# A decoder layer on one core: a third ready-made u tile in each attention head, at other places, and two joints in another order

## The chip, the core and the metric

The kernel runs on one core of a Trainium2 chip. The metric is the device time of one execution in microseconds (us). TensorE is called PE, VectorE DVE, ScalarE ACT, GpSimd POOL and SyncE SP; SP does nothing but issue DMAs here. PE, DVE, ACT and POOL work in parallel, each in its own program order, and wait for each other by semaphores.

## What is computed

```python
h = rms(x, attn_norm_g)
q, k, v, cb, cc, cx = split(h @ w_in[l])             # 512 tokens, D = 2048, float32
a = diff_attention(rms(q), rms(k), v, lam)           # 8 heads, causal, ALiBi
c = cb * causal_conv3(cc * cx)                       # 1024 channels
x = x + concat(rms(a) * (1 - lam_init), c) @ w_out[l]
h2 = rms(x, ffn_norm_g)                              # PEER: 128 x 128 experts, 8 heads, top 16
act = gelu(sum(u[experts] * h2)) * gates
x = x + sum(act * v[experts])
```

Float32 products are made from three float32r products each: an operand is split in a high part (ACT copies it) and a low part (DVE subtracts), and PE multiplies high x high, low x high and high x low.

## The kernel before

**Stages.** In time: the projection to q, k, v (to about 289 us); the head loop, 8 trips of attention together with one eighth of the convolution's projection (to about 620); the output projection (to 800); h2, its transposition and the first queries (to 867); the sweep (to 2219), which multiplies all 128 tiles of 128 experts' u rows with h2 for 384 of the 512 tokens, while DVE does the remaining 128 tokens with gathered rows; and the dense second half with v.

**The u tiles.** A tile is 128 rows of 2048 floats, 1 MB, and must be transposed for PE. In the sweep an ordinary tile is loaded by SP into one of two buffers (`u_tile`), PE turns it in 16 steps of 128 x 128 into PSUM (`turned`, 8 steps after each half of the tile before), ACT and DVE split it from PSUM (`split_u`), and PE multiplies. 56 of the 128 tiles, the odd ones up to 111, are ready-made: in stage one, where DVE is idle at times, SP loads the rows into `near_rows` (or `far_rows`), DVE turns them in four instructions (`turn_rows`) into `near_turned`, and four DMAs of 256 KB (`store_turned`) put the result into `uT_all` in DRAM. The sweep loads such a tile from there, PE turns nothing, and ACT and DVE split it from SBUF. `turned_before(tile)` says which tiles these are. There is one near buffer for rows and one for the turned tile, so a row load waits for the turning before it (`seg_ready`), and a turning waits for its rows (`seg_in`) and for the stores of the one before (`seg_kept` in the heads, where POOL issues the stores, else `seg_stored`).

**A sweep head** is 16 tiles. In heads 0 to 5 PE also makes the queries of a later head, behind tiles 3 to 6 and 9 to 12; DVE chooses the experts of the next head in heads 0 to 6, and does a `dot` and an `add` per tile.

**A trip of the head loop.** PE does the convolution's products, `conv(0)`, `conv(1)`, `conv(2)`, with attention's small products between their parts. The convolution's weights come in six pieces (0 to 5) a head of 512 KB, through two raw buffers `wc_raw`; SP issues piece p + 2 when DVE has split piece p (`wc_ready`). DVE's order is: split piece 3, piece 4, `biased` and `combined` for the four query blocks (scores plus bias and maximum; after ACT's exponentials the combination), split pieces 5 and 0, last combination, split piece 1, norms, `o_n`, `norm_qk`, split piece 2, the conv gate (lines 1461 to 1470). Of the two turnings in a trip, the first is cut in two behind `combined(0)` and `combined(1)`, the second sits between `o_n` and `norm_qk`. SP issues their row loads in

```python
if p in (2, 5):
    next_rows(NEAR, 2 * j + (NEAR_HEADS + p // 5))
```

behind weight pieces 4 and 1. POOL issues in a trip two 1 MB DMAs that fill a grid in DRAM with zeros (`zero_cells`), the head's outputs, the stores of the turned tiles (line 455), and does the roots of the norms. SP's DMAs are queue q1 in the profile, POOL's are q0, ACT's q10.

**The joints.** Into the head loop: ACT splits weight pieces 0, 1 and 2 and then copies two of the four blocks of the last projection chunk (`keep_qkv`), DVE the two others; PE waits for all four before the first convolution product. At h2: PE turns h2 in four blocks of 16 steps (`turn_rows`, line 1797) into PSUM banks 4 to 7, each bank waiting until DVE (`low`) has read the block before.

## Time and profile before

| | us |
|---|---|
| median of 3 runs | 2975.82 (2974.24 to 2977.21) |
| the profiled execution | 2978.89 |
| its span, first to last instruction | 2977.1 |
| PE busy | 2893.4 (97%) |
| DVE busy | 2358.1 (79%) |
| POOL busy | 1518.6 (51%) |
| ACT busy | 1049.6 (35%) |
| moved by DMA | 980.65 MB, 329 GB/s |

Busy times are those of the engines' instructions; matmuls overlap each other, and their ends are modelled, so that a busy PE isn't one at its peak. Idle time is counted just ahead of an instruction and put down to what released it. The share of DMA is the mean busy share of the core's 16 DMA engines.

### The profile page before, as it was taken

How to read it: one execution, taken by the hardware profiler on the slowest of the kernel's cores; microseconds unless marked ns; L12 is line 12 of the kernel's file. 1: busy time of each engine (PE TensorE's matmuls, PEld its weight loads, DVE VectorE, ACT ScalarE, POOL GpSimd, SP SyncE). 2: the span in 40 equal slices, each digit the busy share in tenths (PEclk: the TensorE clock that was granted, in tenths of full speed). 3: DMA queues.
4: the chain of work that ended last, by engine and by line, in shares of the span. 5: the costliest groups of instructions: out<-in, count | busy, mean ns of one | idle time of the engine just before them, and what ended most of it. 6: DMA issues, size and time to landing. Idle time of an engine off the chain costs nothing.

```text
span 2977.1 us, 40581 instructions
## 1 busy us (share of the span) xinstructions
PE 2893.4 (97%) x14993; PEld 2571.8 (86%) x14993; DVE 2358.1 (79%) x3050; ACT 1049.6 (35%) x1373; POOL 1518.6 (51%) x906
## 2 busy tenths in 40 slices
PE   7999999999999999999999999999999999999998
PEld 6887777778889999999999999999998777777777
DVE  6445677755678888988888898899778888899898
ACT  4111433341323343434333343334234333333333
POOL 1000232200015666666666666566868877788752
PEclk9999999999999999999999999999999999999999
DMA  8998777779758998999899898999999999999998
GB/s 298 338 347 273 236 238 236 226 298 314 241 183 304 315 344 296 348 309 331 311 321 339 300 346 312 329 347 355 326 370 390 415 414 414 408 416 416 414 416 343
DMA packets 333295, 980.65 MB, mean 329 GB/s; under 512 B 63764, under 2 KB 180512, under 8 KB 241760
## 3 DMA queue, kind: packets, MB, share of 16 engines
q1 hardware_dynamic: 188560, 508.60, 46.6%
q0 software_dynamic: 107008, 439.75, 41.0%
q10 hardware_dynamic: 37584, 30.43, 3.2%
q8 instruction: 86, 1.41, 0.2%
q14 instruction: 57, 0.47, 0.0%
HBM read 866.33 MB, written 112.33 MB: 329 GB/s over the span
## 4 chain that ended last, share of the span: by engine, by line
PE 63%; DVE 14%; DMA 12%; issue 5%; ACT 3%; POOL 2%; SPq 0%; ACTq 0%; DVEq 0%; POOLq 0%
PE ps L1803 19%; PE ps L1805 19%; PE ps L1804 19%; DMA v_raw<-in_peer_v 9%; PE ps L2053 3%; DVE x_rows L1663 3%; DVE u_row L1654 2%; DMA wc_raw<-in_w_in 2%; DVE v_lo L1703 2%; ACT v_hi L1174 1%; POOL dots L824 1%; POOL v_ring L835 1%; DVE uT_lo L1643 1%; DVE near_turned L1296 1%; DVE uT_lo L1648 1%
## 5 line engine op out<-in xcount | busy, mean ns | idle before, releaser
L1803 PE MATMUL ps<-hT_hi,uT_hi 128*128 128x384 f32 x2048 | 698.9, 341 | 10.5 <-DVE uT_lo L1643 8.8
L1805 PE MATMUL ps<-h2T_lo,uT_hi 128*128 128x384 f32 x2048 | 686.1, 335 | 0.0
L1804 PE MATMUL ps<-hT_hi,uT_lo 128*128 128x384 f32 x2048 | 684.9, 334 | 0.0
L816 POOL DMA_INDIRECT gate_grid<-gates,grid_cells x256 | 547.0, 2137 | 107.4 <-issue 78.8
L1803 PE MATMUL ps<-v_hi,a_hi 128*128 128x512 f32 x1024 | 404.8, 395 | 37.3 <-DVE v_lo L1703 36.6
L1174 ACT ACTIVATE v_hi<-v_raw 128x2048 fp32r<-128x2048 f32 x128 | 245.6, 1919 | 458.3 <-PE ps L1805 348.0
L1804 PE MATMUL ps<-v_hi,a_lo 128*128 128x512 f32 x1024 | 402.9, 393 | 0.0
L1805 PE MATMUL ps<-v_lo,a_hi 128*128 128x512 f32 x1024 | 402.6, 393 | 0.0
L1803 PEld LDWEIGHTS ps<-hT_hi,uT_hi 128*128 128x128 f32 x2048 | 384.8, 188 | 19.1 <-DVE uT_lo L1643 14.8
L1804 PEld LDWEIGHTS ps<-hT_hi,uT_lo 128*128 128x128 f32 x2048 | 385.0, 188 | 1.9
L1805 PEld LDWEIGHTS ps<-h2T_lo,uT_hi 128*128 128x128 f32 x2048 | 384.3, 188 | 0.0
L835 POOL DMA_INDIRECT v_ring<-in_peer_v,experts x128 | 285.5, 2230 | 144.8 <-DVE x_one L1753 113.5
L1703 DVE TENSOR_TENSOR v_lo<-v_raw,v_hi 128x2048 fp32r<-128x2048 f32 x128 | 293.2, 2290 | 74.5 <-ACT v_hi L1174 74.3
L1753 DVE SCALAR_TENSOR_TENSOR x_one<-v_ring,acts,x_one 128x2048 f32<-128x2048 f32 x128 | 300.4, 2347 | 6.9 <-DMA v_ring<-in_peer_v,experts 4.1
L1663 DVE SCALAR_TENSOR_TENSOR x_rows<-v_row,acts,x_rows 128x2048 f32<-128x2048 f32 x128 | 300.0, 2344 | 1.9 <-ACT acts L1127 1.5
L806 POOL DMA_INDIRECT v_row<-in_peer_v,experts x128 | 139.4, 1089 | 315.9 <-DVE x_rows L1663 266.6
L1654 DVE CUSTOM_DVE_ANT_0 u_row<-u_row,h_rows 128x2048 f32<-128x2048 f32 x128 | 292.5, 2285 | 5.9 <-DMA u_row<-in_peer_u,experts 5.9
L824 POOL DMA_INDIRECT dots<-products_one,cells x128 | 258.1, 2016 | 43.4 <-issue 38.7
L1803 PEld LDWEIGHTS ps<-v_hi,a_hi 128*128 128x128 f32 x1024 | 195.0, 190 | 85.7 <-issue 30.1
L1118 ACT ACTIVATE uT_hi<-ps 128x1024 fp32r<-128x1024 f32 x144 | 148.1, 1029 | 310.5 <-PE ps L2053 304.2
L1648 DVE TENSOR_TENSOR uT_lo<-ps,uT_hi 128x1024 fp32r<-128x1024 f32 x144 | 176.1, 1223 | 99.7 <-ACT uT_hi L1118 98.2
L801 POOL DMA_INDIRECT u_row<-in_peer_u,experts x128 | 181.7, 1419 | 123.1 <-DVE dots L1654 49.4
(207 smaller groups left out, 5036.6 us busy)
## 6 DMA issues: line engine op xcount, KB each, us to landing
v_raw<-in_peer_v SPq DMA_DIRECT2D x128, 1024.0 KB, 14.9
u_tile<-in_peer_u SPq DMA_DIRECT2D x72, 1024.0 KB, 7.2
u_tile<-uT_all SPq DMA_DIRECT2D x56, 1024.0 KB, 6.7
near_rows<-in_peer_u SPq DMA_DIRECT2D x40, 1024.0 KB, 8.2
uT_all<-near_turned SPq DMA_DIRECT2D x100, 256.0 KB, 7.0
w_raw<-in_w_in SPq DMA_DIRECT2D x24, 1024.0 KB, 9.1
wc_raw<-in_w_in SPq DMA_DIRECT2D x48, 512.0 KB, 7.4
far_rows<-in_peer_u SPq DMA_DIRECT2D x16, 1024.0 KB, 9.0
```

What stands on the lines that cost most here:

```text
L816: pool.indirect_dma_start(out=gate_grid, out_offset=bass.IndirectOffsetOnAxis(ap=grid_cells[:, d, col:col + 1], axis=0), in_=gates[:, 2 + ...
L824: pool.indirect_dma_start(out=dots[:, s:s + 1], out_offset=None, in_=products_one, in_offset=bass.IndirectOffsetOnAxis(ap=cells[:, col:col ...
L835: pool.indirect_dma_start(out=v_ring[s % RING][:, :], out_offset=None, in_=v_table, in_offset=slot(1, h, s)).then_inc(v_in[s % RING], 16)
L1174: nc.scalar.activation(v_hi[b % 2][:, :], v_raw[b % RAW_RING][:, :], ACT.Copy).then_inc(v_hi_ready, 1)
L1648: v.tensor_tensor(uT_lo[half][:, :, :], ps_uT[half], uT_hi[half][:, :, :].bitcast(F32), ALU.subtract)\
L1654: v.tensor_tensor_reduce(out=u_row[c % 2][:, :], in0=u_row[c % 2][:, :], in1=h_rows[:, 0, :], scale=1.0, scalar=0.0, op0=ALU.mult, op1=ALU ...
L1663: v.scalar_tensor_tensor(out=x_rows[:, 0, :], in0=v_row[c % 2][:, :], scalar=acts0[:, b:b + 1], in1=x_rows[:, 0, :], op0=ALU.mult, op1=ALU ...
L1703: v.tensor_tensor(v_lo[b % 2][:, :], v_raw[b % RAW_RING][:, :], v_hi[b % 2][:, :].bitcast(F32), ALU.subtract).then_inc(v_lo_ready, 1)
L1753: v.scalar_tensor_tensor(out=x_one[:, :], in0=v_ring[s % RING][:, :], scalar=acts[:, s:s + 1], in1=x_one[:, :], op0=ALU.mult, op1=ALU.add) ...
L1803: mm(out, a_hi, b_hi, start=first, stop=False)
L1804: mm(out, a_lo, b_hi, start=False, stop=False)
L1805: return mm(out, a_hi, b_lo, start=False, stop=last)
```

## The change

It makes 63 tiles ready instead of 56. The seven new ones are tile 6 of each sweep head 0 to 6 (`EXTRA_AT = 6`), turned in heads 0 to 6 of the head loop, three near tiles in a trip instead of two. In the trip the first turning is whole and sits behind `combined(1)`; the second sits behind `combined(3)`; the third at the trip's end, behind the conv gate. The row loads are issued behind weight pieces 5, 0 and 1. POOL stores the third one at the beginning of the next trip, ahead of the zero fill. In the sweep, `u_tile[0]` now holds a ready-made tile too. At the first joint ACT splits piece 2 behind its two copies, and PE waits for one of the four blocks at first and for the others ahead of `conv(1)`. At h2, block 1 is turned into banks 0 to 3, after the last output sum has been added from each, and its splits come ahead of the last block's square and mean.

```diff
-KEPT_BY_POOL = 1 + 2 * (HEADS - 1)
+EXTRA = HEADS - 1
+EXTRA_AT = 6
+KEPT_BY_POOL = 1 + 3 * (HEADS - 1)
...
 def turned_before(tile):
-    return tile % 2 == 1 and tile < 2 * TURNED
+    if tile % TOPK == EXTRA_AT:
+        return tile // TOPK < EXTRA
+    return tile % 2 == 1 and tile < 2 * ODD_TURNED
+def kept_row(tile):
+    return ODD_TURNED + tile // TOPK if tile % TOPK == EXTRA_AT else tile // 2
...
+        def turned_bank(n, t, b):
+            return ps[:, b if (n, t) == (1, 1) else 4 + b, :]
...
                     sp.wait_ge(wc_ready, PIECES * j + p + 1)
                     conv_piece(j + (p + 2) // PIECES, (p + 2) % PIECES)
-                    if p in (2, 5):
-                        next_rows(NEAR, 2 * j + (NEAR_HEADS + p // 5))
+                    if p >= 3:
+                        then = (odd_of_head(j, 1), odd_of_head(j, 2), extra(j))[p - 3]
+                        next_rows(3 * j + (NEAR_HEADS + p - 3), then[0])
...
             for j in range(HEADS):
+                if j > 0:
+                    keep_turned(NEAR_HEADS + 3 * j, extra(j - 1))
                 for n in range(2 * j, 2 * j + 2):
                     zero_cells(n)
                 if j > 0:
                     store_o(j - 1)
                 if j < HEADS - 1:
-                    keep_turned(NEAR_HEADS + 1 + 2 * j)
+                    keep_turned(NEAR_HEADS + 1 + 3 * j, odd_of_head(j, 1))
+                    keep_turned(NEAR_HEADS + 2 + 3 * j, odd_of_head(j, 2))
...
-                    keep_turned(NEAR_HEADS + 2 + 2 * j)
...
-            for p in range(PIECE_RING):
+            for p in range(PIECE_RING - 1):
                 split_wc(0, p)
             keep_qkv(chunks - 1)
+            split_wc(0, PIECE_RING - 1)
...
             high(1, 0)
+            high(1, 1)
             square(1, 3)
-            for t in range(1, TB):
+            for t in range(2, TB):
                 high(1, t)
...
                 combined(0)
-                if not last:
-                    turn_rows(NEAR, 2 * j + (NEAR_HEADS + 1), "heads", range(2))
                 biased(2)
                 combined(1)
                 if not last:
-                    turn_rows(NEAR, 2 * j + (NEAR_HEADS + 1), "heads", range(2, 4))
+                    turn_rows(NEAR, 3 * j + (NEAR_HEADS + 1), "heads")
...
                 combined(3)
                 if not last:
+                    turn_rows(NEAR, 3 * j + (NEAR_HEADS + 2), "heads")
                     split_wc(j + 1, 1)
...
                 if not last:
-                    turn_rows(NEAR, 2 * j + (NEAR_HEADS + 2), "heads")
                     norm_qk(j + 1, 1)
...
                 dve.wait_ge(conv_out, j + 1)
+                if not last:
+                    turn_rows(NEAR, 3 * j + (NEAR_HEADS + 3), "heads")
...
             low(1, 0)
+            low(1, 1)
             mean(1, 3)
-            low(1, 1)
...
-            for t in range(TB):
-                pe.wait_ge(proj_kept[t], QKV_CHUNKS)
+            pe.wait_ge(proj_kept[0], QKV_CHUNKS)
...
-                if not first:
+                if first:
+                    for t in range(1, TB):
+                        pe.wait_ge(proj_kept[t], QKV_CHUNKS)
+                else:
                     pe.wait_ge(conv_gated, j)
                 conv(1, 1, 0, 4)
```

Left out are the renamed arguments of the loads and stores (a tile and a row of `uT_all` in place of a count), and the two views of `u_tile`.

## Rows read from the trace of the kernel before

**Rows 1.** Busy time by stage: length, then PE, PEld, DVE, ACT, POOL busy; clock; DMA.
```profile
290.00:330.00 40.00, 37.54 (x174) 29.45 (x175) 23.69 (x57) 14.96 (x31) 9.13 (x11) 0.96 0.65 202
371.00:413.00 42.00, 41.54 (x206) 32.83 (x205) 30.47 (x66) 16.75 (x34) 11.67 (x14) 1.00 0.76 241
790.00:870.00 80.00, 71.71 (x417) 61.29 (x416) 59.27 (x154) 28.51 (x43) 9.34 (x8) 1.00 0.51 180
1210.00:2215.00 1005.00, 998.22 (x5948) 973.23 (x5947) 858.25 (x1240) 373.26 (x596) 654.97 (x387) 1.00 0.94 330
```

**Rows 2.** What PE waited for in the whole span: us, times, longest.
```profile
PE ps L1803 <- DVE uT_lo L1643: 8.8, 14, 1.3
PE ps L1797 <- DVE h2T_lo L1244: 3.6, 2, 2.1
PE ps L1803 <- ACT qkv L900: 3.6, 1, 3.6
```

**Rows 3.** DVE in order of time, one head of the head loop: start, us, instruction.
```profile
378.64 2.48 DVE L1296 STREAM_TRANSPOSE near_turned<-near_rows 128x512 f32<-128x512 f32 x4
383.40 0.69 DVE L1461 TENSOR_TENSOR conv_u<-ps,c_sb 128x512 f32<-128x512 f32 x1
387.67 1.23 DVE L1264 TENSOR_TENSOR wc_lo<-wc_raw,wc_hi 128x1024 fp32r<-128x1024 f32 x1 [0.53 <-DVE b_sb L1470]
400.32 1.30 DVE L1296 STREAM_TRANSPOSE near_turned<-near_rows 128x512 f32<-128x512 f32 x2
420.23 2.48 DVE L1296 STREAM_TRANSPOSE near_turned<-near_rows 128x512 f32<-128x512 f32 x4
```

**Rows 4.** The columns of rows 1, over one quarter of that head.
```profile
387.70:400.30 12.60, 12.14 (x59) 8.81 (x58) 9.15 (x29) 5.73 (x16) 2.61 (x4) 1.00 1.04 382
```

**Rows 5.** ACT in order of time: tile ends in sweep heads 6 and 7.
```profile
1963.70 0.49 ACT L1148 ACTIVATE products<-ps 128x384 f32<-128x384 f32 x1 [3.13 <-PE ps L1805]
1972.92 0.49 ACT L1148 ACTIVATE products<-ps 128x384 f32<-128x384 f32 x1 [3.10 <-PE ps L1805]
...
2109.15 0.50 ACT L1148 ACTIVATE products<-ps 128x384 f32<-128x384 f32 x1 [3.14 <-PE ps L1805]
2119.25 0.50 ACT L1148 ACTIVATE products<-ps 128x384 f32<-128x384 f32 x1 [3.14 <-PE ps L1805]
```

**Rows 6.** The columns of rows 1: tile 6 of head 3; two tiles of head 6.
```profile
1449.00:1461.00 12.00, 12.00 (x69) 11.48 (x68) 9.35 (x17) 2.96 (x5) 7.22 (x5) 1.00 1.02 388
1963.20:1982.30 19.10, 18.71 (x114) 18.33 (x113) 17.99 (x29) 6.05 (x10) 12.51 (x8) 1.00 0.94 347
```

**Rows 7.** DVE in order of time, sweep head 6: second half of tile 6.
```profile
1966.26 1.23 DVE L1648 TENSOR_TENSOR uT_lo<-ps,uT_hi 128x1024 fp32r<-128x1024 f32 x1 [0.28 <-ACT uT_hi L1118]
```

**Rows 8.** SP's issues in order of time: the row load of that head.
```profile
384.37 1.92 SPq L469 DMA_DIRECT2D near_rows<-in_peer_u  x1
```

**Rows 9.** DMA, 393 to 398 us: queues (packets, MB, share); issue, KB, us to landing.
```profile
q0 software_dynamic: 460, 1.77, 87.6%
q1 hardware_dynamic: 449, 0.26, 16.4%
wc_raw<-in_w_in SPq DMA_DIRECT2D x1, 512.0 KB, 9.2
```

**Rows 10.** DMA, 388.5 to 390 us: the weight piece issued just ahead of that.
```profile
wc_raw<-in_w_in SPq DMA_DIRECT2D x1, 512.0 KB, 12.5
```

**Rows 11.** DMA, 449.9 to 451.5 us: row load, weight piece, no POOL traffic.
```profile
near_rows<-in_peer_u SPq DMA_DIRECT2D x1, 1024.0 KB, 7.0
...
wc_raw<-in_w_in SPq DMA_DIRECT2D x1, 512.0 KB, 7.7
```

**Rows 12.** DMA, 403 to 408 us: the stores of a turned tile, alone.
```profile
q0 software_dynamic: 320, 1.05, 81.5%
uT_all<-near_turned POOLq DMA_DIRECT2D x3, 256.0 KB, 4.4
```

**Rows 13.** ACT in order of time: its half of a weight piece's split.
```profile
391.31 1.06 ACT L911 ACTIVATE wc_hi<-wc_raw 128x1024 fp32r<-128x1024 f32 x1 [2.37 <-DMA wc_raw<-in_w_in]
```

More of the change, by code:

```diff
@@ L335, in decoder_layer @@
         ps_key_scores = [ps[:, 7 - c, :].rearrange("p (t n) -> p t n", t=TB) for c in range(2)]
[L336 removed]
+        uT_rows = [u_tile[b][:, :].rearrange("p (a k e) -> p k a e", a=QUADS, e=QUAD) for b in range(2)]
         ps_uT = [ps[:, 2 * i:2 * i + 2, :].rearrange("p b (k e) -> p (b k) e", k=4) for i in range(2)]
@@ L488, in load_qkv_weights, with keep_odd @@
             def load_qkv_weights():
+                def keep_odd(pair, n, last=False):
+                    keep_turned(pair, n, odd(pair, n), None if last else odd(pair, n + 1))
                 def chunk(c, first=False):
@@ L524, in far, with keep_odd @@
                     return FAR_QKV + 2 * c
+                def keep_odd(pair, n, last=False):
+                    seen = EXTRA if pair == NEAR else 0
+                    keep_turned(pair, n, odd(pair, n - seen), None if last else odd(pair, n - seen + 1))
                 for q in range(1, 4):
```

101 lines of the change are left out of this document (54 added, 47 removed).

## The prediction

> **What bounds the kernel now.** I read the busy time by stage first [rows 1]. The reader is to see that PE is the bound nearly everywhere the change works: 41.54 of 42 us in a head of the head loop, 998 of 1005 us in the sweep. DVE is next, 30.47 of 42 and 858 of 1005. Two places leave PE idle, the entry of the head loop (37.54 of 40 us, granted clock 0.96) and the turning of h2 before the sweep (71.71 of 80). What PE waited for [rows 2] names them: 3.6 us for ACT's copy of the projection, 3.6 us in two waits for h2T_lo, and in the sweep 8.8 us for uT_lo of tiles that come ready-made. So a PE instruction removed from the sweep is time won, unless DVE cannot follow; DVE work added to the heads is hidden as long as it, and the transfers it hangs on, fit in 41.6 us, the step from one turning to that of the next head [rows 3]. The DMA engines are the third resource: in a head they are busy for 0.76 of the time on the mean [rows 1], but for 1.04 between 387.7 and 400.3 us [rows 4], which is full.
>
> **Part one, the sweep.** An ordinary tile costs PE 16 turnings, 8 after each half. The step between tile ends is 10.10 us in the last sweep head, where every tile has all 16, and 9.22 us for tile 6 of head 6, whose interval has 8 [rows 5]. So 8 turnings are 0.88 us and a tile 1.76 us. ACT and DVE do the same splits from the tile in SBUF as they did from PSUM. In sweep heads 0 to 5 the intervals of tiles 5 and 6 fall from 12.0 to 11.1 us each, while DVE is busy for 9.35 us in that of tile 6 [rows 6]; it follows, and the whole 1.76 is won. In head 6 it doesn't: DVE is busy 17.99 of 19.1 us over two tiles [rows 6], the gaps between its short instructions fill the rest, and the one real gap is the 0.28 us ahead of tile 6's second half [rows 7]. That gap is what can go there. Sum: 6 x 1.76 + 0.3 = 10.9 us won. The load of tile 8 now waits for DVE's last split of tile 6, some 3 us later than for PE's turnings, and has more than a tile of slack.
>
> **Part two, the heads.** A third tile a head adds to DVE one turning of 2.5 us [rows 3], to DMA 1 MB of rows and 1 MB of stores, and it moves the other two. By DVE's busy time alone, 30.5 + 2.5 of 41.6 us, it is free. But one buffer for rows and one for the turned tile serve all three, so the steps form a loop, and the new places set its order. Per head: turn n1 (ahead of the scores of the fourth block), its four stores, turn n2 (behind the last combination, ahead of the split of weight piece 1 of the next head), SP's row load for n3 and, behind it in SP's order, piece 2 of the next head; its split; the conv gate; turn n3 at the head's end; the split of piece 3; and only then, behind piece 5 in SP's queue, the row load for the next n1. Before, that load was issued one piece earlier, at 384.4, ahead of the full stretch [rows 8]. SP's waits for a turning also hold back the weight pieces now.
>
> What a load costs in the full stretch is in the trace. From 393 to 398 us the POOL queue (q0) moved 460 packets and SP's (q1) 449: one for one, but 1.77 MB against 0.26 MB, since weight pieces go in short packets [rows 9]. The piece issued just before took 12.5 us [rows 10], the next, queued behind it, 9.2 [rows 9]; alone a load and a piece take 7.0 and 7.7 [rows 11]. The Trainium skill (DMA: Bandwidth & Descriptors, Queues, rings and completion order) says the same of every SDMA engine: it goes round the rows of rings that have work, packet by packet. By that rule SP's piece would stay slow for as long as POOL has packets left, the stores of n3 as well as the zero fill, and the rule speaks against these places.
>
> The loop, each term once. Turn n1 2.5. Its stores: 0.3 to the issue, 1.7 of issuing, 4.4 to land [rows 12], and 2.7 more because n2's rows (1.05 MB, at 382 GB/s [rows 4]) share the engines: 9.1; alone 6.4. Turn n2 2.5. Piece 2 behind the rows of n3: 1.1 to its issue and 7.7 [rows 11], plus 2.8 of the 4.1 us of engine time of n2's stores (81.5% of 5 us [rows 12]), which are ahead of it: 11.6; without them 8.8. ACT's and DVE's split of it: 1.06 and 1.23, 2.3 [rows 3, 13]. Conv gate, 383.40 to 387.67: 4.3 [rows 3]. Turn n3 2.5. Split of piece 3 and SP's two issues: 2.0. Rows for n1 behind piece 5: 12.5 + 2.7 - 0.6 (they are issued 0.6 later) = 14.6 [rows 4, 10]; n3's stores are ahead of it as well but the zero fill starts later, so I add only 0.3: 14.9. At best it is the 9.2 of the queued piece [rows 9], at worst all 4.1 of the stores come on top: 18.7. The sum is 2.5 + 9.1 + 2.5 + 11.6 + 2.3 + 4.3 + 2.5 + 2.0 + 14.9 = 51.7 us. With every transfer at its lowest it is 2.5 + 6.4 + 2.5 + 8.8 + 2.3 + 4.3 + 2.5 + 2.0 + 9.2 = 40.5, under the 41.6 of PE; at the highest 55.5.
>
> I take 51.7: no row lets a load behind a weight piece, issued into the zero fill, land in 9.2 us if it has a megabyte of its own. The heads then run at the pace of the loop: +10.1 us in each of the six heads 1 to 6. Heads 0 and 7 hold only a part of the loop, and are taken at nothing. PE would wait in them mostly ahead of the third block of attention weights, since n1 sits between the second combination and the scores of the fourth block. 
>
> **Part three, the joints.** At the head loop's entry PE no longer waits for all four copies and ACT makes them before piece 2. If PE sets the time, the 3.6 us wait and the 1.6 us of low clock go: 5.2. If the loop does, PE's lead is eaten in head 0 and only DVE's start counts; I take 1.0. At h2, block 1 is turned into free banks, so the two waits of 3.6 us shrink, but DVE's four subtractions and scalings stay in series ahead of the queries: between 0 and 3.6, taken 0.6.
>
> **Sum.** 6 x 10.1 = 60.6 lost, 10.9 + 1.0 + 0.6 = 12.5 won: +48.1 us. The profiled execution took 2978.9 us (span 2977.1 and 1.8 around it), 3.1 above the median of 2975.8; it would become 3027.0, and the median 3023.9.
>
> **Rivals.** (A) The steps fit, and it ends faster. This decides at a loop of 41.6 us or less: the loads keep near their lowest bounds, because PE's and POOL's steps slide so that piece 5 no longer meets the zero fill. For it: the lowest sum is 40.5, and DVE has 11 us idle in a head. Against it: 1.04 of DMA share where the load now falls, and 2 MB more a head to move. It gives 10.9 + 5.2 + 0.6 = 16.7 won, 2959.1. (B) Only the queue order of piece 5 bites, all else is at its lowest: 40.5 + 14.9 - 9.2 = 46.2, +4.6 a head, 27.6 in all, net +15.1: 2990.9. (C) The loop passes PE by 2 us a head: 12 lost, 12.5 won, no change: 2975. (D) It doesn't do what it says: the sweep heads behave like head 6 and win 0.3 each, 2.1 in all. The first row of the tile windows speaks against it [rows 6]; it would add 8.8 to any case.
>
> **How the numbers follow.** 0.2%, 6 us, is what a measurement of this kernel can tell from no change. The forecast has 0.64, B 0.16, A 0.13, C 0.07; D is inside them. Slower 0.80, same 0.07, faster 0.13. The range runs from 2972 (a loop just above PE's, between C and A) to 3050 (a loop of 55.5: 6 x 13.9 = 83.4 lost, +70.9, and some clock loss).
>
> **What would show it.** In the changed kernel a head would take about 51 us from one turning to the next of its kind, in heads 1 to 6, and about 41.6 in head 7; DVE would be idle ahead of near_turned, released by the row load (n1) and by the stores (n2); PE idle, 60 us in all, released by DVE's probs and by splits; row loads issued behind piece 5 would take some 15 us to land. Sweep heads 0 to 5 would be 1.76 us shorter, head 6 by 0.3. Heads of 41.6 us would make the forecast wrong, and a row load landing in under 10 us would say why.

## The result, and the profile after

The changed kernel takes 3000.7 us (median of 4 runs, 2994.8 to 3001.5) against 2976.5 for the one before on the same chip (4 runs, 2974.2 to 2978.4). The ratio is 1.0074, with a 95% interval from 1.0062 to 1.0085: 22 us slower. The forecast was 3023.9, slower by 48. The side was right and the size was twice too large. The loop that the forecast describes is the one at work in the heads; one term of it was too large.

The profiled execution has a span of 2999.6 us (2977.1 before). I cut both spans at four points that are easy to find in PE's order of time: the first turning of qk_n (head 0), the first matmul of the output projection, the first of the sweep and the end of its last. An execution is one sample; the code of the last stage is the same in every kernel here, and that stage took from 749.7 to 757.7 us in their traces, so a difference of a few us there means nothing.

```
stretch, us                              before    after    change   forecast
start to the first qk turning             305.1    299.4      -5.7      -1.0
to the output projection (8 heads)        320.0    360.6     +40.6     +60.6
to the first sweep matmul                 242.0    243.2      +1.2      -0.6
first to last sweep matmul               1352.2   1340.7     -11.6     -10.9
last stage                                757.7    755.7      -2.0       0
span                                     2977.1   2999.6     +22.5     +48.1
```

So the sweep gave what it was to give, and most of the difference from the forecast, 20 of 25.6 us, lies in the heads. By head, from one first qk turning to the next, they are longer by 4.1 us in head 0 (45.0 instead of 40.9), by 34.3 in heads 1 to 6 together (5.7 each) and by 2.2 in head 7. The entry seems to have given more than forecast, but head 0 takes 4.1 of its 5.7 us back. Here are the stretches by the columns of [rows 1]: the entry, one head from the turning of n3 to the next, the turning of h2, the sweep.

```profile
290.00:330.00 40.00, 37.95 (x186) 29.50 (x186) 27.02 (x61) 15.30 (x31) 11.07 (x15) 1.00 0.75 219
392.52:440.14 47.62, 43.22 (x203) 33.29 (x202) 32.62 (x71) 16.10 (x32) 14.01 (x18) 0.96 0.78 253
810.00:890.00 80.00, 74.78 (x408) 63.41 (x407) 51.88 (x116) 29.30 (x40) 7.54 (x8) 0.98 0.43 135
1245.00:2243.00 998.00, 990.51 (x5873) 965.59 (x5872) 858.83 (x1237) 373.28 (x595) 640.85 (x387) 1.00 0.95 334
```

The entry has lost its low clock (0.96 in [rows 1], 1.00 here) and its 3.6 us wait. One head takes 47.6 us, where it took 41.6; PE is busy for 43.2 of them at a clock of 0.96, DVE for 32.6, and the DMA share on the mean is 0.78, hardly more than the 0.76 of [rows 1]. No engine is full in a head any more, so something waits. What PE waited for (us, times, longest), which answers [rows 2]:

```profile
PE ps L1933 <- DVE probs L1452: 21.4, 16, 2.5
...
PE ps L1940 <- ACT aT L1002: 10.8, 7, 2.0
PE ps L1841 <- DVE h2T_lo L1280: 1.8, 1, 1.8
```

Two entries are new or grown: probs, 2.2 us before, and aT, which wasn't there. Both lie wholly in the heads. In the head of the second line of the first fence PE's long waits are at the first block's probs and at the fourth block's aT; between them come six matmuls that start 0.43 us apart instead of 0.23 (busy 0.63 instead of 0.40, PE in order of time):

```profile
400.72 0.33 PE L1933 MATMUL ps<-ident,probs 128*128 128x128 f32 x1 [1.99 <-DVE probs L1452]
...
404.01 0.63 PE L1842 MATMUL ps<-hT_hi,wc_lo 128*128 128x512 f32 x1
...
406.49 0.40 PE L1842 MATMUL ps<-hT_hi,wc_lo 128*128 128x512 f32 x1
...
423.17 1.16 PE L1940 MATMUL ps<-qkv,aT 128*128 x8 [1.63 <-ACT aT L1002]
```

DVE and SP in the same head (start, us, instruction; idle before it and what ended that), which answer [rows 3] and [rows 8]:

```profile
392.52 2.49 DVE L1332 STREAM_TRANSPOSE near_turned<-near_rows 128x512 f32<-128x512 f32 x4 [0.25 <-DVE b_sb L1504]
...
408.10 2.49 DVE L1332 STREAM_TRANSPOSE near_turned<-near_rows 128x512 f32<-128x512 f32 x4 [3.04 <-DMA near_rows<-in_peer_u]
...
420.30 2.49 DVE L1332 STREAM_TRANSPOSE near_turned<-near_rows 128x512 f32<-128x512 f32 x4 [1.55 <-DMA uT_all<-near_turned]
...
435.01 1.23 DVE L1300 TENSOR_TENSOR wc_lo<-wc_raw,wc_hi 128x1024 fp32r<-128x1024 f32 x1 [2.11 <-ACT wc_hi L945]
...
440.14 2.49 DVE L1332 STREAM_TRANSPOSE near_turned<-near_rows 128x512 f32<-128x512 f32 x4 [0.25 <-DVE b_sb L1504]
```

```profile
397.09 0.36 SPq L494 DMA_DIRECT2D near_rows<-in_peer_u  x1
...
410.79 0.34 SPq L494 DMA_DIRECT2D near_rows<-in_peer_u  x1
...
422.99 0.35 SPq L494 DMA_DIRECT2D near_rows<-in_peer_u  x1
423.88 12.90 SPq L593 DMA_DIRECT2D wc_raw<-in_w_in  x3
```

n3 is turned at 392.5, n1 at 408.1, n2 at 420.3, n3 again at 440.1. The row load for n1 is issued at 397.1, for n2 at 410.8, for n3 at 423.0; behind the last stands weight piece 2, at 423.9. Its load takes 10.0 us, and the row load for n1 takes 10.9 (issues: KB, us to landing):

```profile
near_rows<-in_peer_u SPq DMA_DIRECT2D x1, 1024.0 KB, 10.9
...
wc_raw<-in_w_in SPq DMA_DIRECT2D x1, 512.0 KB, 10.0
```

The steps of my sum, by these rows: n1 2.5 (2.5 forecast), its stores until n2 starts 9.7 (9.1), n2 2.5, from its end to n3 17.4 (11.6 + 2.3 + 4.3 = 18.2), n3 2.5, from its end to n1 13.1 (2.0 + 14.9 = 16.9). That makes 47.6 where I had 51.7. It is the loop that I described, with one link 3.8 us shorter.

Adding up to the period proves nothing by itself, since any list of steps that closes on itself does, idle time included. What counts is that no step has slack. The profile's chain of the work that ended last (start, us, what) goes through the head before in this way, some of its pieces:

```profile
349.75 10.50 DMA near_rows<-in_peer_u
...
361.00 1.87 DVE near_turned L1332 x3
...
364.81 7.62 DMA uT_all<-near_turned
...
373.08 1.87 DVE near_turned L1332 x3
...
376.03 10.24 DMA wc_raw<-in_w_in
...
391.58 0.70 DVE b_sb L1504
```

That is the forecast's list: rows for n1, n1, its stores, n2, weight piece 2, the conv gate's last step, and then n3. This is head 1. No PE instruction is in its chain, and none in those of three others of the six heads 1 to 6; in heads 2 and 3 the chain takes a way of the same length over PE for 8.8 us, while the rows of n1 land 0.1 us before it is turned there too. The waits of DVE in all heads (us, times, longest):

```profile
DVE near_turned L1332 <- DMA near_rows<-in_peer_u: 15.7, 6, 3.0
...
DVE near_turned L1332 <- DMA uT_all<-near_turned: 12.4, 8, 2.4
```

n1 is turned within 0.2 us of the landing of its rows in six heads of seven (in head 4 n3's stores land last), n2 within 0.1 us of n1's last store in all seven, piece 2 is issued 0.7 to 1.1 us behind n2's end, and n3 follows the gate by 0.25 us each time. PE, busy for 43.2 of 47.6 us, has 4 us a head to spare, and its waits are where they show.

### The profile page after: what moved, and what is told of

It is laid out like the page before. It is cut to its first block, busy times and chain, and to the rows that moved or that the text cites. A ratio compares the mean times of both kernels' runs of the same rounds, so it can differ in the third digit from the quotient of the medians.

```text
span 2999.6 us, 40476 instructions
## 1 busy us (share of the span) xinstructions
PE 2889.1 (96%) x14881; PEld 2562.0 (85%) x14881; DVE 2373.3 (79%) x3078; ACT 1049.2 (35%) x1373; POOL 1528.3 (51%) x934
## 3 DMA queue, kind: packets, MB, share of 16 engines
q0 software_dynamic: 109248, 447.09, 40.9%
## 4 chain that ended last, share of the span: by engine, by line
PE 61%; DVE 16%; DMA 15%; issue 5%; ACT 2%; POOL 1%; SPq 0%; ACTq 0%; DVEq 0%; POOLq 0%
PE ps L1841 19%; PE ps L1843 19%; PE ps L1842 19%; DMA v_raw<-in_peer_v 9%; DVE x_rows L1699 3%; PE ps L2093 3%; DVE u_row L1690 3%; DMA wc_raw<-in_w_in 2%; DMA uT_all<-near_turned 2%; DVE v_lo L1739 2%; DVE near_turned L1332 1%; ACT v_hi L1210 1%; DMA near_rows<-in_peer_u 1%; DVE uT_lo L1679 1%; DVE uT_lo L1684 1%
## 5 line engine op out<-in xcount | busy, mean ns | idle before, releaser
L850 POOL DMA_INDIRECT gate_grid<-gates,grid_cells x256 | 536.3, 2095 | 108.7 <-issue 78.8
L840 POOL DMA_INDIRECT v_row<-in_peer_v,experts x128 | 147.4, 1152 | 318.1 <-DVE x_rows L1699 275.4
L858 POOL DMA_INDIRECT dots<-products_one,cells x128 | 271.5, 2121 | 40.9 <-issue 38.7
L480 POOL DMA_DIRECT2D uT_all<-near_turned x88 | 49.2, 567 | 425.7 <-DVE near_turned L1332 422.2
L1841 PE MATMUL ps<-w_hi,hT_hi 128*128 128x512 f32 x624 | 243.7, 390 | 1.9 <-DVE wi_lo L1286 1.9
L1842 PE MATMUL ps<-w_hi,hT_lo 128*128 128x512 f32 x624 | 243.4, 390 | 0.0
## 6 DMA issues: line engine op xcount, KB each, us to landing
v_raw<-in_peer_v SPq DMA_DIRECT2D x128, 1024.0 KB, 15.4
```

The lines of the kernel that those rows point to most:

```text
L840: pool.indirect_dma_start(out=v_row[b % 2][:, :], out_offset=None, in_=v_table, in_offset=slot(0, i, b)).then_inc(v0_in[b % 2], 16)
L850: pool.indirect_dma_start(out=gate_grid, out_offset=bass.IndirectOffsetOnAxis(ap=grid_cells[:, d, col:col + 1], axis=0), in_=gates[:, 2 + ...
L858: pool.indirect_dma_start(out=dots[:, s:s + 1], out_offset=None, in_=products_one, in_offset=bass.IndirectOffsetOnAxis(ap=cells[:, col:col ...
L1841: mm(out, a_hi, b_hi, start=first, stop=False)
L1842: mm(out, a_lo, b_hi, start=False, stop=False)
```

## The experiments

Three theories stood at the start. **T1**, the forecast's: the three tiles pass through one rows buffer and one turned buffer, and this loop of transfers, with weight piece 2 and the conv gate in it, sets the length of a head. **Order**: the new places alone cost PE waits, loop or no loop. **Contention**: the engines have too much to move in a head. A fourth, T2 to T4 in the expectations, came out of the first runs: PE sets the length, and waits for engines that weight pieces hold up. Where a sum is given for "the heads", it is the second line of the table above, read in the same way from the run's own trace.

**The joints alone** (e1). The kernel before, with the entry of the heads and the turning of h2 in the changed order and nothing else:

```diff
-            for p in range(PIECE_RING):
+            for p in range(PIECE_RING - 1):
                 split_wc(0, p)
             keep_qkv(chunks - 1)
+            split_wc(0, PIECE_RING - 1)
...
-            for t in range(TB):
-                pe.wait_ge(proj_kept[t], QKV_CHUNKS)
+            pe.wait_ge(proj_kept[0], QKV_CHUNKS)
...
-                    if t > 0:
-                        pe.wait_ge(hT_ready, 4 * (n * TB + t - 1) + b + 1)
+                    if (n, t) == (1, 1):
+                        pe.wait_ge(out_added[b], OUT_CHUNKS)
+                    elif t > 0:
+                        pe.wait_ge(hT_ready, 4 * (n * TB + (0 if (n, t) == (1, 2) else t - 1)) + b + 1)
```

> The kernel before with the two reordered joints of stage one and of h2 alone, no third tile, old places. Three theories. T (PE sets the pace of the heads, so what the entry saves is kept): in the changed kernel the first qk turning came 5.7 us earlier and the stretch from the first h2 turning to the first sweep matmul was 1.2 us longer; here the same two, so 2976.5 - 5.7 + 1.2 = 2972.0, ratio 0.9985. As forecast (the two joints are worth 1.0 and 0.6): 2974.9, ratio 0.9995. Rival (DVE's start of head 0 sets the pace, the entry's gain is eaten within a head): first qk turning 5 us earlier, but wo first matmul where it was; ratio 1.000 or 1.0004.

Measured 0.9975 (0.9965 to 0.9985), 7 us faster. The first qk turning comes 5.3 us earlier, the heads take 320.9 us (320.0 before), the next stretch 241.6 (242.0). PE sets the pace of the heads before, so the entry's gain is kept whole. What the h2 joint is worth can't be told: 0.4 us here, -1.2 in the changed kernel, while the kernels below, all with the same h2 order, took 241.4 to 243.2 in their traces.

**The third tile left out of the heads** (e2), and **the third tile on DVE alone** (e3). With both, the sweep reads the kept rows of tile 5 once more where it would read those of tile 6. In e2 the two other tiles keep their new places:

```diff
-                    if p >= 3:
-                        then = (odd_of_head(j, 1), odd_of_head(j, 2), extra(j))[p - 3]
-                        next_rows(3 * j + (NEAR_HEADS + p - 3), then[0])
+                    if p in (3, 4):
+                        next_rows(2 * j + (NEAR_HEADS + p - 3), odd_of_head(j, p - 2)[0])
...
-                if not last:
-                    turn_rows(NEAR, 3 * j + (NEAR_HEADS + 3), "heads")
```

and e3 keeps DVE's turning, with no load and no store behind it, so that it waits for those of n2 alone; the row load for the next n1 still waits for it:

```diff
-                    turn_rows(NEAR, 3 * j + (NEAR_HEADS + 3), "heads")
+                    turn_rows(NEAR, 3 * j + (NEAR_HEADS + 3), "heads", loaded=2 * j + (NEAR_HEADS + 2),
+                              kept=2 * j + (NEAR_HEADS + 3))
```

> The changed kernel without the third tile's making: in the heads it is neither loaded nor turned nor stored; tile 6 of a sweep head then reads the kept rows of tile 5 once more, so that part of the output is wrong. The two other tiles stay at their new places, joints and sweep as in the changed kernel. T (the loop of the three tiles through one rows buffer and one turned buffer sets the heads' length): heads back at 41.6 us or less, the 40.6 us lost between the first qk turning and the first output-projection matmul go, total 2976.5 - 5.7 + 1.2 - 11.6 = 2960. Rival 1 (the new places of the two tiles put their turnings ahead of the scores' readers and cost PE waits by themselves): heads of 43 to 45 us, total 2970 to 2985. It also prices the sweep alone: -11.6 us from first to last sweep matmul (forecast 10.9).

> As the run before, but DVE makes the third turning at the head's end (2.5 us) from the rows it last turned; no load and no store for it, so SP's row load for n1 still waits for that turning and stands behind piece 5, and no tile 6 is kept. T: what costs is that three tiles pass the two buffers with their transfers; with two passes left the heads stay at PE's pace, 41.6 to 42.2 us, total 2960 to 2964. Rival 1 (DVE's order: the turning at the head's end delays the conv split and the first probs of the next head, PE waits 2 us for them and falls to the low clock for 6 matmuls, as in the trace of the changed kernel): heads of 45 to 47 us, total 2985 to 2995.

e2 measured 1.0003 (0.9993 to 1.0012), its heads 340.0 us; e3 1.0041 (1.0025 to 1.0057), its heads 350.4. T1 wanted 320 to 325 for both. So the theory of the order is right as far as it goes: with the changed kernel and e1 the runs give 320.9 with the old places, 19.1 more with the new places of two tiles, 10.4 more with the third turning on DVE, 10.2 more with the third tile's own transfers. The ratios say the same: e2 lies 0.67% above e1 less the sweep's gain (0.9975 - 0.0039), e3 0.38% above e2, the changed kernel 0.33% above e3, 20, 11 and 10 us. These are the prices in this order of adding, and not three shares of the changed kernel's heads: a wait that costs in e2 costs nothing where a longer chain covers it, as e6 and e7 will show. Nor is e3's step the price of DVE's 2.5 us a head alone, since DVE also waits longer for the rows of n1 there (12.7 us in seven heads; in e2 3.8 in five); no run parts the two.

What the new places do can be read in e2. First PE's wait and ACT in order of time in e2, then ACT at the same step of the kernel before:

```profile
PE ps L1934 <- ACT aT L999: 14.7, 7, 2.6
```

```profile
416.79 1.06 ACT L942 ACTIVATE wc_hi<-wc_raw 128x1024 fp32r<-128x1024 f32 x1 [6.03 <-DMA wc_raw<-in_w_in]
417.75 0.58 ACT L999 ACTIVATE aT<-ps 128x512 f32<-128x512 f32 x1
```

```profile
412.00 1.06 ACT L911 ACTIVATE wc_hi<-wc_raw 128x1024 fp32r<-128x1024 f32 x1 [3.15 <-DMA wc_raw<-in_w_in]
412.97 0.58 ACT L967 ACTIVATE aT<-ps 128x512 f32<-128x512 f32 x1
```

aT of the fourth block stands in ACT's order behind the split of weight piece 1 of the next head. Before, that load was issued at 408.2, as the last of n1's stores landed, and took 3.8 us; in e2 n1 is turned later, its stores and n2's rows are on their way, and piece 1, issued at 410.1, takes 6.7. Against the first qk turning of the head (387.0 before, 389.6 in e2) it is issued no later and lands 2.2 us later, and PE waits 2.0. In e3 the same wait is 19.1 us in seven heads, and probs 4.1.

**SP's row load for n1 ahead of weight piece 5** (e4). This takes the very link that I had put at 14.9 us:

```diff
-                    if p >= 3:
-                        then = (odd_of_head(j, 1), odd_of_head(j, 2), extra(j))[p - 3]
+                    if p in (2, 4, 5):
+                        n = max(p - 3, 0)
+                        then = (odd_of_head(j, 1), odd_of_head(j, 2), extra(j))[n]
```

> The changed kernel with SP's row load for n1 issued behind weight piece 4 and ahead of piece 5, as soon as n3 is turned (before: 2.0 us later and behind piece 5). T (the loop sets the pace, this load is one link of it): n3's end to n1's start falls from 13.1 us to about 8.5, the step from n3 to n3 from 47.4 to about 43, total 3000.7 - 7 x 4.4 = about 2970. Rival 2 (the engines are full there and n3's four stores stand ahead of the load anyway): the load takes 12 us instead of 10.9, the step falls by 1 us at most, total 2993 to 3000. Rival 3 (the loop isn't the limit; PE's waits for probs and aT are): the step stays at 47.

The load lands in 6.5 us instead of 10.9, n1 no longer waits for its rows, and the time hardly moves: 1.0061 (1.0044 to 1.0077), an interval that overlaps the changed kernel's, the heads 361.2 us, the step from n3 to n3 47.5. A DMA row and DVE in the same head:

```profile
near_rows<-in_peer_u SPq DMA_DIRECT2D x1, 1024.0 KB, 6.5
```

```profile
405.79 2.49 DVE L1333 STREAM_TRANSPOSE near_turned<-near_rows 128x512 f32<-128x512 f32 x4 [0.68 <-DMA uT_all<-near_turned]
...
420.01 1.30 DVE L1333 STREAM_TRANSPOSE near_turned<-near_rows 128x512 f32<-128x512 f32 x2 [0.95 <-DMA uT_all<-near_turned]
```

The loop has not gone, it has taken its other way: n1 needs its rows and also the turned buffer, and n3's stores land at 405.8, as n1 starts. From n3 to n1 it takes 12.9 us instead of 15.6; from n1 to n2 14.2 instead of 12.2, since n1's stores, which now run beside pieces 5 and 0 and n2's rows, take up to 9.8 us instead of 7.7; from n2 to n3 20.4 instead of 19.8. The chain of the work that ended last has PE in it in one of the six heads 1 to 6 only, for 7 us. So this run does not speak against T1; the expectation's rival 2, n3's stores ahead and a step shorter by 1 us at most, is what happened, though with a quick load. The link that I had put at 14.9 has a second one beside it, nearly as long, and here the next transfer pays for what the first has saved.

**SP's row load for n3 behind weight piece 2** (e5), **ACT's aT ahead of the split of piece 1** (e6, and e7, which is e2 with it):

```diff
-                for p in range(PIECES):
+                for p in range(1, PIECES + 1):
...
-                    if p >= 3:
+                    if p in (3, 4, 6):
+                        n = {3: 0, 4: 1, 6: 2}[p]
```

```diff
+                keep_aT(3)
                 if not last:
                     split_wc(j + 1, 1)
                 else:
                     split_mix(0)
-                keep_aT(3)
```

> The changed kernel with one SP step in another order: the row load for n3, and SP's wait for n2's turning ahead of it, stand behind weight piece 2 of the next head instead of ahead of it. Theory T2, formed on the runs before (the heads are not paced by the loop of the three tiles but by PE, which waits twice a head for engines that weight pieces hold up; one of the two is piece 2, issued 6 us late behind the wait and landing after 10.5 us, so that the conv gate, n3's turning and the first probs come late): piece 2 is issued 6 us earlier and lands before 427 us of the head that the old one had it at 434; the gate is no longer late, PE's wait for the first probs (2.0 us, and 1.5 us of low clock behind it) goes or falls to 0.5, heads of 44 to 45 us, total 3000.7 - 7 x 3 = 2980, range 2975 to 2988. T1 (the loop of transfers is the limit): n3's rows come 4 us later, the loop is as long as before or longer, total 3000 to 3010.

> The changed kernel with two steps of ACT in another order: the copy of the fourth block's turned weights (aT) ahead of the split of weight piece 1 of the next head. T2 (the second of PE's two waits is for this copy, which ACT can make only when piece 1 has landed, late, because n1's stores and n2's rows now fall onto that load): PE's waits for aT (10.8 us in seven heads) go to under 2, total 3000.7 - 9 = 2992; less if the other wait takes part of it. T1 (the loop): PE waits elsewhere instead, the total stays at 2998 to 3002.

> The kernel without the third tile's making (tile 6 reads tile 5's kept rows again, that part of the output is wrong) with the same two steps of ACT in the other order. In the run without the third tile and the old order the heads still took 19 us more than before and PE's only large wait was 14.7 us for aT. T2: this wait goes and with it the clock's fall behind it, the heads are back at PE's 320 to 322 us, total 2979 - 18 = 2961. Rival (the new places cost DVE or PE elsewhere, the wait only shows it): the time moves by under 5 us, 2974 or more.

e5 measured 1.0028 (1.0018 to 1.0038), its heads 348.9 us: 11.7 less than in the changed kernel. It takes a link out of the forecast's loop: piece 2 is issued at 416.0 instead of 423.9 and no longer waits for n2, and the step from n2 to n3 falls from 19.8 to 17.9 us. The T1 of the expectation, with a loop as long as before or longer, had n3's rows in it; but in the changed kernel they land at 429.0 and n3 is turned at 440.1, behind piece 2 and the gate, as the forecast has it. So the gain is one of the loop as much as of T2, which also wanted it. e6 parts the two: T2 wanted 9 us, T1 none. e6 measured 1.0075 (1.0058 to 1.0092), no gain; its heads 359.8. e7 measured 0.9964 (0.9950 to 0.9978), its heads 328.5 against e2's 340.0. What PE waited for from 290 to 660 us, in e5 and then in e6:

```profile
PE ps L1943 <- ACT aT L1005: 15.4, 7, 2.9
PE ps L1936 <- DVE probs L1455: 7.9, 9, 1.5
```

```profile
PE ps L1933 <- DVE probs L1452: 21.2, 17, 2.5
PE ps L1956 <- ACT o_mix L989: 9.4, 7, 2.0
```

In e5 the waits for probs shrink from 21.4 to 7.9 us and those for aT grow from 10.8 to 15.4. In e6 those for aT are gone, and ACT's next step, o_mix behind the splits of pieces 2 and 3, makes PE wait 9.4 us. The same two steps of ACT change nothing in the changed kernel and give 11.5 us without the third tile: PE's wait for aT is on the path in e2 and beside it in the changed kernel, where the loop leaves PE 4 us a head in any case. The theory formed on the first runs, that the loop doesn't set the heads, was wrong for this kernel.

e7 also shows the price that I had put on the row load for n1, once. In its second head the load stood behind piece 5 and was issued just after the zero fill:

```profile
near_rows<-in_peer_u SPq DMA_DIRECT2D x1, 1024.0 KB, 14.8
```

```profile
359.71 1.90 DVE L1329 STREAM_TRANSPOSE near_turned<-near_rows 128x512 f32<-128x512 f32 x3 [6.62 <-DMA near_rows<-in_peer_u]
```

14.8 us, DVE idle for 6.6, PE for 5.1 and then at the low clock: this head took 48.2 us. But in the same place behind the same two fills the thirteen other row loads of e7 and e2 took 9.5 to 11.8 us; what made this one longer isn't known. In the changed kernel n3's four stores are ahead of the fill in POOL's queue. Queues (packets, MB, share of 16 engines' time) of the changed kernel from 397 to 404 us:

```profile
q0 software_dynamic: 220, 0.70, 55.7%
q1 hardware_dynamic: 1087, 0.91, 42.8%
```

POOL's queue moves 0.70 MB in 7 us there, 100 GB/s, and SP's 0.91, where [rows 9] had 1.77 MB against 0.26 in 5 us. I had seen that "the zero fill starts later", and had kept the 12.5 us of a piece beside the fill all the same.

**The zero fill out of the heads** (e8), 12 fills of 1 MB:

```diff
-                for n in range(2 * j, 2 * j + 2):
+                for n in range(2 * j, 2 * j + 2) if j in (0, HEADS - 1) else ():
                     zero_cells(n)
...
             norm(1)
+            for n in range(2, 2 * HEADS - 2):
+                zero_cells(n)
```

> The changed kernel with the 12 zero fills of heads 1 to 6 (1 MB each) issued after the heads, behind the norm of h2, where the DMA share is 0.43. In the changed kernel they queue behind n3's stores on POOL and piece 0 of the next head takes 16 us beside them. T1 (transfers are the limit, two megabytes a head fewer): piece 0 lands in 7 to 8 us, heads fall by 3 us or more, total 2975 to 2980. T2 (PE waits for piece 1 and piece 2, which don't meet the zero fill): piece 0 lands 8 us earlier, the heads' length falls by under 1 us each, total 2994 to 3001, and it may lose 1 to 3 us ahead of the sweep.

The heads took 357.9 us, 2.7 less, for 2 MB less in each of six heads. The row loads for n1 take 10.4 to 10.7 us there with no fill in the head at all, so the fill had hardly a part in their 10.9. Contention with the fill, the third theory, is not what sets the heads: with a sixth of a head's bytes gone (253 GB/s over 47.6 us are 12 MB) PE still waits 13.5 us for probs and 15.4 for aT. What the loop's own transfers cost each other is another matter, and inside its links. The total, 1.0144 (1.0127 to 1.0161), is a miss of both expectations: the fills cost 22 us where they now are (265.5 us from the output projection to the sweep instead of 243.2). PE's longest wait from 850 to 930 us, and the queues from 858 to 870:

```profile
PE ps L2055 <- ACT pqT L1109: 16.6, 2, 15.9
```

```profile
q0 software_dynamic: 1015, 3.90, 89.4%
q1 hardware_dynamic: 1013, 0.52, 14.3%
```

PE is busy for 54 of those 80 us at a clock of 0.85. SP's loads for the first choice of experts (keys and query weights) come in packet for packet with the fills, 1013 against 1015, and get 0.52 MB in 12 us beside 3.90.

**The three orders together** (e9), then **n3 turned ahead of the conv gate** (e10), which also stores n3 at once:

```diff
                     norm_qk(j + 1, 1)
+                    turn_rows(NEAR, 3 * j + (NEAR_HEADS + 3), "heads")
                     split_wc(j + 1, 2)
...
                 dve.wait_ge(conv_out, j + 1)
-                if not last:
-                    turn_rows(NEAR, 3 * j + (NEAR_HEADS + 3), "heads")
...
-                if j > 0:
-                    keep_turned(NEAR_HEADS + 3 * j, extra(j - 1))
...
+                if j < HEADS - 1:
+                    keep_turned(NEAR_HEADS + 3 + 3 * j, extra(j))
                 pool.wait_ge(conv_out, j + 1)
```

> The changed kernel with three steps in another order: SP's row load for n1 ahead of weight piece 5, its row load for n3 (and the wait for n2's turning) behind piece 2 of the next head, and ACT's copy of the fourth block's turned weights ahead of the split of piece 1. One at a time they moved the heads by +1.0, -11.5 and -0.6 us, since the next late step took over. T3 (the heads are held by several chains of nearly the same length through weight pieces 1 and 2, so that a remedy pays only together with the others): together 20 to 28 us, heads of 333 to 341 us between the first qk turning and the output projection (360.6 in the changed kernel, 320.0 in the one before), total 2973 to 2981. T1 (a loop of transfers of 47 us sets the heads whatever the order): no better than the 2986 of the second remedy alone.

> As the run before, and n3 is turned ahead of the split of piece 2 and of the conv gate (not at the head's end), its stores issued at once, ahead of the store of the conv branch. T3: the 2.5 us of DVE ahead of the first probs of the next head go, and n3's stores and n1's rows start some 8 us earlier; PE's waits for probs and aT fall from 32 us to under 8, heads of 322 to 330 us, total 2961 to 2970: faster than both kernels. T1: a loop of 47 us less the 8 us is under PE's 41.6, so the same result; the two theories part only in the run before. Rival (n3's turning waits for n2's stores on DVE and delays the split of piece 2 and the gate): heads no shorter than in the run before.

e9 measured 0.9998 (0.9988 to 1.0009), its heads 337.7 us, 22.9 less than in the changed kernel, where the three remedies one at a time gave -0.6, 11.7 and 0.8. With piece 2 no longer behind n2, the two others, which gave nothing alone, bring 11.2 us more. The T1 of the expectation, no better than e5, took the loop for closed whatever the order, and was wrong. e10 measured 1.0089 (1.0072 to 1.0106), its heads 359.6; its total was to be 2961 to 2970, and is 3002. The load of weight piece 4, first in the changed kernel and then in e10, and DVE and PE in e10:

```profile
wc_raw<-in_w_in SPq DMA_DIRECT2D x1, 512.0 KB, 3.9
```

```profile
wc_raw<-in_w_in SPq DMA_DIRECT2D x1, 512.0 KB, 9.3
```

```profile
399.64 1.22 DVE L1303 TENSOR_TENSOR wc_lo<-wc_raw,wc_hi 128x1024 fp32r<-128x1024 f32 x1 [4.36 <-ACT wc_hi L948]
```

```profile
403.67 0.47 PE L1935 MATMUL ps<-ident,probs 128*128 128x128 f32 x1 [4.56 <-DVE probs L1455]
```

n3's stores, 7.5 us earlier against the head's first qk turning (389.8 in the changed kernel, 390.2 here), now fall onto piece 4, whose load takes 9.3 us instead of 3.9. DVE waits 4.4 us for ACT's part of its split, which stands ahead of the first probs, and PE waits 4.6. The loop has slack here: n1's rows land at 401.8, and it is turned at 408.5.

**The split of piece 4 behind the first combination**, added to e9 (e11) and to e10 (e12):

```diff
-                split_wc(j, 4)
                 exps(0)
                 exps(1)
+                split_wc(j, 4)
...
-                split_wc(j, 4)
...
                 biased(1)
                 combined(0)
+                split_wc(j, 4)
```

> The kernel of the three reordered steps, and the splits of weight piece 4 (ACT's and DVE's) behind the first combination of each head instead of ahead of its first probs. In the kernel of the three steps PE still waited 9.8 us for probs and 5.4 us for pieces of wc_lo in the heads. T4 (what stands between n3's turning and the first probs on DVE is one of the chains that set the heads): 1.3 us leave that chain, the probs waits at the head's start go; heads of 331 to 335 us instead of 337.7, total 2970 to 2974. Against it: piece 0 of the next head is then issued 5 us later and may be what PE waits for next, total 2977 to 2982.

> The kernel of the run before with n3's turning also ahead of the split of piece 2 and of the conv gate. Without the later split of piece 4 this order took 3002: n3's four stores were issued together with piece 4, whose load took 9.3 us instead of 3.8, DVE waited 4.4 us for it ahead of the first probs and PE 4.6 us for those, each head. T4: with the split of piece 4 behind the first combination the probs don't wait for the load any more, the 29.7 us of PE's waits in eight heads go to under 8, and the clock's fall behind them; heads of 323 to 330 us, total 2962 to 2969. Rival (the chain through the buffers, T1, or piece 4 now late for the third convolution): heads of over 335 us, total over 2974.

e11 measured 0.9986 (0.9975 to 0.9997), its heads 336.0: 1.7 us less than e9's in the traces, 3.6 by the ratios, whose intervals overlap, and a smaller gain than I expected (331 to 335). e12 measured 0.9959 (0.9947 to 0.9971): 12 us faster than the kernel before, 34 faster than the changed one. Its heads take 328.8 us. The columns of [rows 1] over one head, what PE waited for from 290 to 660 us, and DVE's turnings in that head:

```profile
381.90:424.80 42.90, 41.87 (x209) 33.20 (x208) 33.27 (x71) 15.84 (x32) 13.51 (x18) 1.00 0.86 281
```

```profile
PE ps L1935 <- DVE probs L1454: 8.2, 10, 1.6
PE ps L1942 <- ACT aT L1005: 1.4, 1, 1.4
```

```profile
381.94 2.49 DVE L1335 STREAM_TRANSPOSE near_turned<-near_rows 128x512 f32<-128x512 f32 x4 [0.29 <-DMA uT_all<-near_turned]
...
399.66 2.49 DVE L1335 STREAM_TRANSPOSE near_turned<-near_rows 128x512 f32<-128x512 f32 x4
...
412.83 2.49 DVE L1335 STREAM_TRANSPOSE near_turned<-near_rows 128x512 f32<-128x512 f32 x4 [1.25 <-DMA uT_all<-near_turned]
...
424.78 2.49 DVE L1335 STREAM_TRANSPOSE near_turned<-near_rows 128x512 f32<-128x512 f32 x4 [0.36 <-DMA uT_all<-near_turned]
```

Three tiles pass through the same two buffers in 42.8 us (381.94 to 424.78), at a DMA share of 0.86, with PE busy for 41.9 and its clock at 1.00. e10 and e12 differ only in where one weight piece is split (1.06 us of ACT's work and 1.23 of DVE's, done in both), and in no turning and no order of transfers; yet their heads differ by 30.8 us. So the two buffers as such don't ask for 47 us a head, and once n3 stands ahead of piece 2's split and of the gate, which cuts the forecast's loop, the order of the weight pieces is what counts. It says nothing against the loop in the changed kernel, where these steps are in it.

## Why the prediction was right or wrong

**The sweep** was right: -11.6 us for -10.9. Heads 0 to 5 are shorter by about 1.8 us each and head 6 by 0.7, where I had 0.3.

**The entry of the heads.** I had two values, 5.2 if PE sets the time and 1.0 if the loop does, because then "PE's lead is eaten in head 0". With the old places it was kept (5.3 in e1). In the changed kernel the first qk turning came 5.7 us earlier and head 0 grew by 4.1: 1.6 are left at head 1, near the 1.0 taken, and as forecast. **The h2 joint**, forecast 0.6, is too small to be seen.

**The heads: the mechanism was right.** "The heads then run at the pace of the loop" holds in the changed kernel. Its steps follow each other without slack in the trace; taking out the wait of piece 2 for n2 (e5) took 11.7 us off; taking PE's waits for aT away (e6) took nothing off. The forecast also named that wait ("SP's waits for a turning also hold back the weight pieces now"). Its signs came out too: DVE idle ahead of near_turned for the rows (n1) and for the stores (n2), PE idle for probs and splits.

**The step that failed is one term of the sum**: "Rows for n1 behind piece 5: 12.5 + 2.7 - 0.6", with 0.3 added 14.9. The load took 10.9 us in the head read above, and 10.3 to 10.9 in five of heads 1 to 6 (7.4 in the other, where n3's stores came last). The 2.0 in front of it was 2.1. The base of the term, 12.5, is what piece 5 took beside the zero fill in the kernel before. No row load in this place paid as much, but one: behind n3's stores 10.9 at most, with no fill in the head 10.4 to 10.7 (e8), behind the fill without those stores 9.5 to 11.8, and 14.8 once (e2, e7). The other links were right within 1 us: the stores of n1 9.7 for 9.1, from n2 to n3 17.4 for 18.2. So the loop is 47.6 us there (47.4 on the mean of six) and not 51.7. In six heads the one term makes 24 us, of the 26 by which they missed (34.3 for 60.6). Heads 0 and 7, taken at nothing, grew by 4.1 and 2.2.

**What the sum didn't see.** It charged the new places through the loop alone. e2 shows that they cost 19.1 us with no third tile at all, through the late piece 1 ahead of aT. And "by DVE's busy time alone ... it is free" is reading a mean: DVE is busy for 30 of 42 us, but from the conv gate to the first probs (387.1 to 396.4 before) it has 3 us idle, and PE waits 0.5 us at the end of it already. In the changed kernel the loop covers the first (e6); what the second adds there isn't shown. But with a loop of 41.6 us or less the heads would not have come back to 41.6: in e2 heads 1 to 6 take 42.5 to 45.4.

**The queues.** Of the Trainium skill's rule for the engines (DMA: Bandwidth & Descriptors, Queues, rings and completion order), that they go round the rows of rings with work packet by packet, the trace after shows no one for one: 220 packets of POOL's queue against 1087 of SP's from 397 to 404 us, where [rows 9] had 460 against 449. Where only fills stand in POOL's queue the trace does show it, 1015 against 1013 in e8. Whether that queue was short of packets for a part of those 7 us, no run here shows.

**Where PE waits** was wrong in the place, "mostly ahead of the third block of attention weights": of 32.2 us (60 forecast), 12.7 are for the first block's probs, 10.8 for the fourth block's aT, 4.5 for the fourth's probs and 4.2 for the third's. **The clock** came out as forecast, "the slow matmuls lie beside the loop and cost little": heads 2 to 4, with a granted clock of 0.96, take 47.8, 47.1 and 47.0 us, heads 5 and 6, at 1.00, 47.2 and 47.9.

**The rivals.** B (2990.9) was nearest in size, nearer than the forecast, by luck: it kept the one term that was too large and put the stores and piece 2, which were right in the forecast's sum, at their lowest. A said that the steps could fit if the loads kept clear of one another; e12 comes near it in time, at 2966 against the 2959 I gave it, but by five reordered steps that the change does not make, and e2 shows that its heads of 41.6 us were not to be had with these places.

## What to carry to other kernels

A list of steps through a shared buffer that closes on itself always adds up to the period. It is the bound if each step starts as the one ahead of it ends, head after head; read that first, in the waits of the engine that turns and in the chain of the work that ended last. Then take a link out (e5). Shortening one is a weaker test: a second link beside it, here the stores of the same buffer beside the rows, can take its place, and the time stays (e4). A wait of PE's is worth removing only where it is on that chain: the same edit gave 0.8 us beside the loop and 11.5 without it.

When a transfer's price is taken from a trace, take it from one with the same traffic ahead of it: the 12.5 us of a piece beside a fill were the wrong row for a load behind four stores. And before a transfer or its wait is moved in hand-ordered queues, list the small loads that it will now run beside or stand ahead of: here a 512 KB weight load went from under 4 us to between 6 and 10, and each engine that splits it does a more urgent step only after it. Remedies must be tried together: alone they gave 11.7, 0.8 and -0.6 us, together 22.9, and a fourth and fifth, which with those three brought it to 31.8, cost 22 us when one of them was left out (e10).

## What the hardware showed that I had not expected

The 512 KB weight load landed in 3.6 to 3.9 us alone (piece 4 of the changed kernel), in 6.3 to 7.0 beside four 256 KB stores and a 1 MB row load (its piece 1), in 9.3 behind stores issued with it (e10), and in 16.6 us beside stores, a row load and the zero fill (piece 0), where without the fill it took 11.2 to 11.4 (e8). A 1 MB row load took 5.8 to 6.5 us at best, 10.3 to 10.9 beside n3's stores, and behind the zero fill 9.5 to 11.8 thirteen times and 14.8 once (e2, e7).

PE fell to the lower clock level behind quite short waits, but not behind each. Of seven waits of 1.8 to 2.5 us in the changed kernel's heads four (1.84, 1.99, 2.05, 2.48) were followed by six to eight matmuls 0.43 us apart and three (1.98, 2.13, 2.31) by none; in e5 three of 2.5 to 2.9 us were followed by five to seven and one of 2.0 by none, in e11 one of six of 1.64 us by seven, and in e10 those of 3.8 to 5.5 us all by three to seven. With six slow steps a wait of 2 us keeps PE busy 1.2 us longer.

What stays open: why POOL's queue moved only 0.70 MB in 7 us while its stores and fills were pending, and what made one row load of e7 take 14.8 us. e12's heads are still 7.9 us longer than e1's (328.8 against 320.9); its trace shows 6.5 us more of PE's waits there (9.6 against 3.1), and removing those was not tried.
